# Two more first-projection chunks held in ring slots 10 and 11, in place of two query chunks

## What is computed

```python
def conformer_conv_module(h, w_pw1, b_pw1, w_dw, b_dw, ln_g, ln_b, w_pw2, b_pw2):
    a = h @ w_pw1 + b_pw1                      # 1024 -> 2048
    a = a[..., :D] * sigmoid(a[..., D:])
    y = depthwise_conv(a, w_dw, width=31) + b_dw
    y = silu(layer_norm(y, ln_g, ln_b))
    return y @ w_pw2 + b_pw2

def peer_ffn(h, w_q, sub_keys, u, v):
    q = (h @ w_q).reshape(T, 8, 2, 128)        # w_q: 1024 x 2048
    ...                                        # top 16 of 128 keys twice, top 16 of the 256 sums
    hb = einsum('td,tkd->tk', x, u[ids])       # 128 picks a token
    act = gelu(hb) * gate
    return einsum('tk,tkd->td', act, v[ids])
```

## Time and profile before

| | |
|---|---|
| median of 3 runs | 1567.49 us (1563.81 to 1574.69) |
| the profiled execution | 1567.84 us, of which the span of the profile is 1566.1 us |
| VectorE busy | 1101.3 us, 70% |
| TensorE matmul busy | 1057.7 us, 68% |
| GpSimd busy | 710.1 us, 45% |
| ScalarE busy | 514.7 us, 33% |
| DMA traffic | 611.75 MB, mean 391 GB/s |
| of it gathers | 536.90 MB |

### The profile page before, as it was taken

How to read it: one execution, slowest core, us unless ns; L and a number is a source line. 1 busy time by engine, 2 the same in 40 slices (tenths; PEclk the granted TensorE clock), 3 DMA queues, 4 the chain that set the end, 5 groups by cost and what they waited for, 6 DMA issues and landing times.

```text
span 1566.1 us, 20662 instructions
## 1 busy us (share of the span) xinstructions
PE 1057.7 (68%) x6966; PEld 528.1 (34%) x6966; DVE 1101.3 (70%) x2839; ACT 514.7 (33%) x1569; POOL 710.1 (45%) x566
## 2 busy tenths in 40 slices
PE   7999857666674576667746678646767657565655
PEld 7796433332331143323413335312433313111111
DVE  2745567787887678986448889899558878654455
ACT  3222314333232444324313443434243234322223
POOL 0002434344444366675334436575444445454552
PEclk9999978888787788887768889967887879778686
DMA  9147999999999999999999999999999999999996
GB/s 381 55 145 269 372 421 421 420 420 421 418 413 420 416 389 422 416 392 422 421 421 396 406 380 421 420 422 417 420 421 421 420 418 418 410 422 421 421 421 272
DMA packets 85451, 611.75 MB, mean 391 GB/s; under 512 B 9440, under 2 KB 10208, under 8 KB 12640
## 3 DMA queue, kind: packets, MB, share of 16 engines
q0 software_dynamic: 73728, 536.90, 83.2%
q1 hardware_dynamic: 11472, 73.26, 11.6%
q10 hardware_dynamic: 144, 0.26, 0.0%
HBM read 609.34 MB, written 1.05 MB: 390 GB/s over the span
## 4 chain that ended last, share of the span: by engine, by line
DMA 76%; PE 13%; DVE 7%; ACT 2%; issue 1%; DVEq 1%; ACTq 0%; POOL 0%; SPq 0%; POOLq 0%
DMA ring<-experts_dram,idx_now 75%; PE pm L1239 6%; PE side L1491 3%; DVE ring L1042 2%; PE side L1239 2%; DMA ring<-wq_dram 1%; DMA x_tok<-x_dram 0%; PE pm L1380 0%; ACT diag_all L663 0%; PE side L1462 0%; DVE top_i L962 0%; DVE x_tok L1056 0%; DVE onehot L963 0%; DVE top_i L978 0%; DVE conv_buf L1111 0%
## 5 line engine op out<-in xcount | busy, mean ns | idle before, releaser
L498 POOL DMA_INDIRECT ring<-experts_dram,idx_now x512 | 692.5, 1353 | 708.8 <-DMA ring<-experts_dram,idx_now 421.2
L1491 PE MATMUL side<-ring,diag_all 64*64 64x512 f32 x2056 | 650.8, 772 | 476.6 <-ACT diag_all L663 468.0
L1042 DVE SCALAR_TENSOR_TENSOR ring<-ring,h_tok 128x1024 f32<-128x1024 f32 x512 | 611.1, 1224 | 249.5 <-DMA ring<-experts_dram,idx_now 242.7
L1491 PE MATMUL pm<-ring,diag_all 64*64 64x512 f32 x2040 | 647.5, 773 | 0.0
L1491 PEld LDWEIGHTS side<-ring,diag_all 64*64 64x64 f32 x2056 | 153.1, 162 | 897.4 <-ACT diag_all L663 646.6
L654 ACT ACTIVATE ge<-hb 128x2 f32<-128x2 f32 (+1 forms) x257 | 52.4, 204 | 830.7 <-DVE ring L1042 830.3
L663 ACT ACTIVATE diag_all<-ident,act_v 128x64 f32<-128x64 f32 x512 | 150.7, 341 | 21.3 <-issue 0.4
L1491 PEld LDWEIGHTS pm<-ring,diag_all 64*64 64x64 f32 x2040 | 151.7, 162 | 0.0
L657 ACT ACTIVATE act_v<-ge,gates 128x1 f32<-128x1 f32 x512 | 123.5, 288 | 17.7
L1111 DVE SCALAR_TENSOR_TENSOR conv_buf<-conv_buf,chan_sb 128x128 f32<-128x128 f32 x480 | 128.9, 348 | 0.0
L1239 PEld LDWEIGHTS side<-h_t,wbuf 128*128 128x128 f32 x448 | 52.3, 195 | 13.3 <-issue 10.6
(11 more groups left out here) (207 smaller groups left out, 967.4 us busy)
## 6 DMA issues: line engine op xcount, KB each, us to landing
wbuf<-wq_dram SPq DMA_DIRECT2D x16, 1024.0 KB, 9.2
wbuf<-w_dram SPq DMA_DIRECT2D x16, 1024.0 KB, 9.7
ring<-w_in_dram SPq DMA_DIRECT2D x5, 2048.0 KB, 22.5
wbuf<-w_o_dram SPq DMA_DIRECT2D x8, 1024.0 KB, 5.3
ring<-experts_dram,idx_now POOLq DMA_INDIRECT x512, 11.6
ring<-wq_dram SPq DMA_DIRECT2D x6, 1024.0 KB, 11.9
ring<-w_dram SPq DMA_DIRECT2D x4, 1024.0 KB, 9.2
gain<-gains_dram SPq DMA_DIRECT2D x7, 512.0 KB, 12.6
```

Of the source, the lines that this page charges most:

```text
L498: pool.indirect_dma_start(ring[:, r, :], None, table[layer], bass.IndirectOffsetOnAxis(idx_now[:, i % 2, n - n0:n - n0 + 1], 0)) \
L1042: dve.scalar_tensor_tensor(out=ring[:, slot, 0:D], in0=ring[:, slot, 0:D], scalar=1.0, in1=h_tok[:, t, :], op0=ALU.mult, op1=ALU.mult, acc ...
L1491: step = pe.matmul(acc[odd][c][j * HALF:(j + 1) * HALF, :], diag[rows, r % (2 * BATCH), :], ring[rows, slot, D + c * COLS:D + (c + 1) * COLS],
```

## The change

Slots 10 and 11 keep w1 chunks 4 and 5 from pick 128 to pick 311, in place of layer 1's query chunks 4 and 5 from pick 224 to 403. These two query chunks now pass through `wbuf`, once for each tile; w1 chunks 4 and 5 no longer do. Slots 12 and 13 come back at pick 312 and no longer at 300. The picks have 14 slots before pick 128, 10 for picks 128 to 311, 14 for 312 to 423, and 16 after. SyncE's order changes in the places that the diff shows.

```diff
 KEPT = [("q", 0, 2, 14), ("q", 0, 3, 15), ("w1", 0, 0, 14), ("w1", 0, 1, 15), ("w1", 0, 2, 12), ("w1", 0, 3, 13),
-        ("q", 2, 4, 10), ("q", 2, 5, 11), ("q", 2, 6, 14), ("q", 2, 7, 15)]
+        ("w1", 0, 4, 10), ("w1", 0, 5, 11), ("q", 2, 6, 14), ("q", 2, 7, 15)]
-AWAY = {10: (PICKS + 6 * RING, 3 * PICKS + RING + 4), 11: (PICKS + 6 * RING, 3 * PICKS + RING + 4), 12: (PICKS, 2 * PICKS + 2 * RING + 12), 13: (PICKS, 2 * PICKS + 2 * RING + 12), 14: (RING - 2, 3 * PICKS + 2 * RING + 8), 15: (RING - 2, 3 * PICKS + 2 * RING + 8)}
+AWAY = {10: (PICKS, 2 * PICKS + 2 * RING + 24), 11: (PICKS, 2 * PICKS + 2 * RING + 24), 12: (PICKS, 2 * PICKS + 2 * RING + 24), 13: (PICKS, 2 * PICKS + 2 * RING + 24), 14: (RING - 2, 3 * PICKS + 2 * RING + 8), 15: (RING - 2, 3 * PICKS + 2 * RING + 8)}
...
             load_gain("bias", 0)
-            for c in range(4):
+            for c in range(6):
                 load_kept("w1", 0, c)
-            load_chunks("w1", 0, 4, KD)
+            load_chunks("w1", 0, 6, KD)
             load_gain("norm", 5)
             load_chunks("w2", 0, 0, 4)
             load_chunks("q", 2, 0, 2)
             load_gain("norm", 6)
-            load_chunks("q", 2, 2, 4)
-            for c in (4, 5):
-                load_kept("q", 2, c)
+            load_chunks("q", 2, 2, 6)
             load_gain("bias", 1)
             for c in (6, 7):
                 load_kept("q", 2, c)
-            load_chunks("w1", 1, 4, KD)
+            load_chunks("w1", 1, 6, KD)
             load_gain("norm", 7)
             load_chunks("w2", 1, 0, 4)
             load_chunks("q", 3, 0, 2)
             load_gain("norm", 8)
-            load_chunks("q", 3, 2, 4)
+            load_chunks("q", 3, 2, 6)
```

## The result

The changed kernel takes 1571.63 us in the median of 22 runs (1565.8 to 1575.34); the kernel before, beside it, 1568.73 (1563.81 to 1574.69). The ratio, taken over all runs of both, is 1.0023, 95% interval 1.0014 to 1.0032, which is 2.2 to 5.0 us. The forecast was +2.8 us, within a range of 1561 to 1581. Weighted by the inverse squares of the half widths the two make 1.0017, give or take 0.0007: +2.6 us, 1.5 to 3.8. But the two lie 0.0019 apart, more than the 0.0016 that their intervals allow together, so the true uncertainty is wider than this. The change makes the kernel a little slower; that it is slower at all rests mainly on the first comparison. The profiled execution took 1573.54 us with a span of 1571.8, so the two profiles are 5.7 us apart, more than the medians.

What follows compares the result with a forecast made beforehand. From about 175 us the bound was bytes over 421 GB/s, plus 16.3 us lost below that rate. Terms +4 - 2.3 + 1.5 - 0.4 = +2.8 us against 1567.84 (median 0.3 less): 1570, range 1561 to 1581.

Steps and rivals of the forecast that it cites:

- Bytes: Loads through `wbuf` and to kept slots: 40 chunks and 10 loads before and after, so nothing changes.
- Ten slots alone: Second phase with 10 slots: five of 96 gathers come late, all within 5.9 us of cover; cost 0.
- Term A: Second phase: 6.2 us of loads pulled forward from 603 to 627, VectorE's lag grows; +4 us (0 to +8).
- Term B: End of second phase: query chunks and bias pushed back to about 827 to 850, filling holes; -2.3 us (-6.2 to 0).
- Term C: Third phase: loads gone from 976 to 990, VectorE's lag grows with 10 slots until pick 311; +1.5 us (0 to +4).
- Term D: From pick 312: 14 slots where there were 12, little to win; -0.4 us (-0.5 to 0).
- The sum: Whole kernel: +4 - 2.3 + 1.5 - 0.4 = +2.8 us, giving 1570.
- The throttle rival: Slots throttle the whole second phase, with GpSimd's waits for TensorE several times 9.8 us: +16.8, 1584; chance 0.13.
- The port rule: During taps: VectorE holds the port pair it shares with GpSimd, delaying gathers' descriptors; term A nearer its upper end.

Runs made afterwards that it cites:

- the first comparison: The changed kernel timed beside the kernel before: ratio 1.0023 (1.0014 to 1.0032); timed so a second time, 1.0004 (0.9991 to 1.0017).
- the second profile of the changed kernel: Profile from timing the unaltered changed kernel once more against the kernel before: ratio 1.0004 (0.9991 to 1.0017).
- the held loads: Second phase's w1 chunks 6 and 7 held until 4 and 5 are used: on the changed kernel 0.9993; with slots back early 0.9982, 6.3 us under those slots alone.
- late query chunks: Kernel before, with layer 1's query chunks 4 and 5 loaded only after the products of query chunks 2 and 3: ratio to before 0.9982.
- slots back early: Changed kernel with slots 12 and 13 back at pick 292, 10 and 11 at 300: ratio to before 1.0022, once more 0.9998.
- the narrow taps: 30 of 31 taps done on 8 of 128 columns: ratio to before 0.9983 in the kernel before, 0.9980 in the changed kernel.
- third phase held: Changed kernel with tile 1's w1 chunks 6 and 7 held back until chunks 4 and 5 are used: ratio to before 1.0041.
- six in flight: Six gathers in flight in place of five: ratio to before 1.0012 in the changed kernel, 0.9977 in the kernel with late query chunks.

## Why the prediction held, step by step

**Bytes: right.** 611.75 MB in both profiles.

**Ten slots alone: right**, 0.9996, and the trace fits its mechanism, late gathers within the cover of the queue: the waits for slots grew from 9.8 to 15.8 us, most of them at the first gathers of the phase, and the holes did not grow.

**Term A: the mechanism right, the size small.** 4 us was forecast. The lag came as said, 7 us at the taps for 6.2 forecast. The holes from 560 to 705 grew from 6.0 to 12.0 us, 6.0 (5.1 in the second profile of the changed kernel); the held loads were worth 6.3 us in time. What was off is the sum over single gathers: it took before's issue times, added 6.2 us to each release, and counted the worst overrun, at 196, as the whole loss. The profile shows release waits in pair after pair, nine between 630 and 705, 25.6 us together, where before had two, 1.6 us together; once the slots bind, each pair's wait adds. The upper bound of that term, 8, had named this. Nearly all of the 6.2 us of traffic taken out of the taps was lost.

**Term B: right, and too small.** 2.3 us forecast. In the changed kernel the stretch from 785 to 925 lost 3.9 us in place of 7.5 (1.1 of it from 785 to 835, which its second profile does not show), and 2.8 us came out in time when done alone. The first part went as forecast: from 835 to 860 before lost 2.4 us, and nine of the ten profiles with late query chunks and full taps lose 0.1 at most. For the second part the forecast was that the holes remain. After 860 the changed kernel lost 2.8 us and not 5.1, but over the ten profiles it is 2.8 to 6.3, and 5.6 and 2.9 in two profiles of one and the same kernel (slots back early). So these runs do not tell whether that step failed. From 835 to 925 the ten lose 2.8 to 6.4 us together; the two with the query chunks early lose 7.5 and 8.3.

**Term C: too small in the profile, unsettled in time.** 1.5 forecast, 4.4 in the profile at 990 to 1030, from nothing to some 4 in time. The reason given, fewer slots until 311 on a larger lag, is shown for the hole by the early slots closing it in both their profiles.

**Term D: too small to tell.** 0.4 us was forecast. From 1030 to 1280 the rate is 420 before and 421 after; one step of the rate is 0.6 us there, and kernels with the same slots stand between 419 and 421.

**The sum** of +2.8 beside 2.6 to 3.6 is closer than its terms deserve, and that is luck. A was under by 2, C by up to 3, B by 0.5 in time and 1.3 in the profile on the other side. In the profiles the terms come to 6.0 - 3.6 + 4.4 - 0.6 = 6.2 us, which fits the 5.7 between the two spans and is twice the forecast; the medians are 2.9 apart.

**The throttle rival** was half right. Its mark, GpSimd's waits for TensorE several times 9.8 us, came: 49.6. What did not hold is that it would last: after 705 the waits are 4.0 us and the rate is 421 in both kernels; the last taps start at 686.6 and 693.6. Some of the waits do lie away from the taps, at the start of the phase: 12.7 us from 510 to 560, where it was 5.2. **The port rule** of the Trainium skill (SBUF — State Buffer, "SBUF: two separate sides") would have put A toward its upper end. The size came out there, but hardly for that reason: from 630 to 705 GpSimd's instructions, all but one of them gathers, were shorter in the changed kernel (42.39/27 = 1.57 us each) than before (54.19/30 = 1.81), and of the nine that had waited for a slot two took over 3 us. The section also has a condition that the prediction left out. What keeps GpSimd from writing descriptors is, by the Trainium skill, a VectorE instruction in a 2-port mode; one with two SBUF inputs, as a tap and a dot have, holds up only a GpSimd instruction that reads SBUF.

That VectorE holds up the gather instruction is shown nevertheless, more closely than by the narrow taps alone (36.71/29 = 1.27 us each). Here taps, dot, the end of the dot and a gather in the kernel before:

```profile
669.02 4.30 DVE L1111 SCALAR_TENSOR_TENSOR conv_buf<-conv_buf,chan_sb 128x128 f32<-128x128 f32 x16
671.54 3.72 POOL L498 DMA_INDIRECT ring<-experts_dram,idx_now  x1 [0.30 <-issue]
673.22 1.23 DVE L1042 SCALAR_TENSOR_TENSOR ring<-ring,h_tok 128x1024 f32<-128x1024 f32 x1
674.36 0.10 DVE L1042 DVE_READ_ACCUMULATOR ring<-ring,h_tok 128x1 f32 x1
```

The gather ends at 671.54 + 3.72 = 675.26, 0.90 us after the dot is over and the read of its sum begins. In the timelines it is so for every gather of more than 1.15 us from 560 to 705: 31 before, 30 in the changed kernel, 44 in the kernel before with narrow taps, and each ends 0.88 to 0.91 us after such a read begins. So a gather that is held is let go at the end of a dot, also where it began during the taps. Not every gather during the taps is held: the one at 670.22 took 1.01 us. Which port or lock does this, no run shows.

## What to carry to other kernels

Where DMA sets the time, what a load costs depends on the stretch in which it runs. Here 6.2 us of traffic taken out of the stretch that VectorE limits was lost nearly whole (6.0 us of hole), since nothing filled its place. So before keeping a block in place to save its second load, look in which stretch that load runs: here the saved w1 loads ran at the start of the third phase's taps (932 us), and the query loads that paid for them run at 1197 and 1211, where DMA is the limit. Moving loads from a stretch where VectorE waits for landings into one where the slots bind gained 2.8 us, with one added line and no change of the slots. And two profiles show where time moves, but a hole of 4.5 us in them need not be in the median.

## What the runs showed that was not expected

TensorE's granted clock is 0.63 from 655 to 695 in the changed kernel and 0.79 before, in a stretch where it did 116 matmuls in place of 148; more of its time was at 1.2 GHz and less at 2.4. That would lengthen the release of a pair just where the slots bind. But over 630 to 705 the clock is 0.73 in the changed kernel and 0.80, 0.86 and 0.86 in three variants with the same hole (early slots, third phase held, six in flight), against 0.82 before. So a lower clock is not needed to make the hole.

The hole from 630 to 705 repeats from profile to profile far better than the run time, which differs by 6 to 11 us between executions of one kernel: the changed kernel and its variants with the loads pulled forward lost 8.4, 7.8, 8.2, 8.7, 8.0 and 9.4 us there, all others with full taps 1.8 to 3.2. The holes after 860 do not repeat so well, as said under term B.
